# Stick-breaking attention inside a two-layer encoder: from one head at a time to pairs of heads

## The chip, the cores and the metric

One core of a Trainium2 chip runs the whole kernel. The metric is the device time of one execution in microseconds (us); the figure compared is the median of several executions. TensorE is called PE in the profile (PEld is its weight loads), VectorE is DVE, ScalarE is ACT, GpSimd is POOL.

## What is computed

An encoder trunk of two layers over 272 tokens (16 learned ones and 256 frames), 1024 channels, batch 1, all in float32. Each layer is SwiGLU feed-forward, a token mixer, SwiGLU feed-forward, each with an RMSNorm before and after. The mixer of the first layer is stick-breaking attention, the mixer of the second is sliding-window attention. Only the first is touched by the change:

```python
z = einsum('bqhd,bkhd->bhqk', q, k) * HEAD_DIM ** -0.5          # 16 heads of 64 channels
visible = k_pos[None, :] < q_pos[:, None]
log_stay = where(visible, log_sigmoid(-z), 0.0)
log_pass = cumsum(log_stay, axis=3, reverse=True) - log_stay
w = where(visible, exp(log_sigmoid(z) + log_pass), 0.0)
o = einsum('bhqk,bkhd->bqhd', w, v)
```

Before it stands a projection of the 1024 channels to queries, keys and values, behind it an output projection.

## The kernel before, in words

The five engines have one program each; they meet at semaphores. Channels lie on the 128 partitions and tokens along the free axis. The large projections (`in_panel`, `out_panel`) multiply weights that are split into a high and a low part, three matmuls for each block of 128 by 128 (`three`, L887 to L889). All matmuls of the attention itself are plain float32, and each of these calls appears in the profile as two weight loads and two matmuls.

The stick-breaking stage lies between `in_panel` and `out_panel` of the second sub-layer. Its score matrix is kept with keys on the partitions: three blocks of keys (`SB_KEY`), each with the queries that can see them, 272, 144 and 128 columns of which 432 (`SB_W`) are used. For one head:

- TensorE `scores(h)` (L1003 to L1014): three matmuls over the 64 channels of the head, that is, over half of the partitions (`r`, the upper or the lower half by the parity of the head). They write PSUM bank `h % 2` and signal `z_done`. Two calls in flight: it waits until VectorE has read head h-2 (`z_ready`).
- VectorE: `z = SCALE * scores + mask` (L702), then `e = min(-z, z) = -|z|` (L709).
- ScalarE: `e = exp(e)` (L483), `e = ln(1 + e)` (L490).
- VectorE: `sp = max(z, 0) + e` (L718), the softplus of z.
- TensorE `running_sums(h)` (L1016 to L1034): six matmuls of `sp` with a triangle of ones or with ones, over all 128 partitions, into bank `2 + h % 2`; signals `c_done`.
- VectorE: `w = z - sums` (L732); ScalarE: `w = exp(w)` (L487).
- TensorE `values(h)` (L1036 to L1052): three matmuls of `w` with the head's 64 value columns, which fill the upper or lower half of the output partitions of bank `4 + h // 2 % 2`; signals `o_done`.
- For each two heads, ScalarE copies the output to `y_hi` (L494) and VectorE takes the rest `y_lo` (L737), for the output projection.

The order is written out by hand as steps. In step `st` TensorE does `scores(st)`, `running_sums(st - 2)`, `values(st - 4)` (L1066 to L1072). VectorE does `z(st)`, `e(st)`, `sp(st - 1)`, `w(st - 3)`, and in every second step a `y_lo`. ScalarE does `exp(e, st)`, `exp(w, st - 3)`, `ln(st)`, and in every second step a `y_hi`. So the `sp` that `running_sums` of a step reads was made in the step before. Ahead of the steps, TensorE does `scores(0)`, `scores(1)` and 24 transposes of the values (L1062), which ScalarE (L478) and VectorE (L725) copy to `v_tok`.

GpSimd clears the padding columns of `sp` and `w` (L374, L375).

Of the kernel before, what the change touches and what calls it, by code (L numbers as in the profile page):

```python
# [25 lines left out]
P = 128  # L26
# [31 lines left out]
SB_PAD = P - 16  # L58

# [64 lines left out]
def build(nc, x_in, meta_in, norm_g, w_gate, w_up, w_down, sb_w_in, sb_w_out,  # L124
          swa_w_in, swa_sinks, swa_w_out, const_in, out):
    ctx = ExitStack()
    with ctx:
# [36 lines left out]
        with ExitStack() as over:  # L164
            def mix_sb(name, shape, dt=F32):
                return over.enter_context(nc.sbuf_tensor(name, shape, dt))
            qkv = mix_sb("qkv", [P, 3 * KT, L])
            v_tok = mix_sb("v_tok", [P, 3, D])
            z = mix_sb("z", [P, 4, SB_W])
            e = mix_sb("e", [P, 2, SB_W])  # L170
            sp = mix_sb("sp", [P, 2, SB_PAD + SB_W])
            w = mix_sb("w", [P, 3, SB_PAD + SB_W])
        with ExitStack() as over:
# [15 lines left out]
            inv = swa_sb("inv", [P, 2, 2, GROUP])  # L189

# [180 lines left out]
        def _(pool):  # L371

            pool.wait_ge(proj_drained, 1)
            nc.gpsimd.memset(sp[:, :, 0:SB_PAD], 0.0).then_inc(pad_zero, 1)  # L374
            nc.gpsimd.memset(w[:, :, 0:SB_PAD], 0.0).then_inc(pad_zero, 1)  # L375
# [26 lines left out]
        def _(a):  # L402
# [51 lines left out]
            for t in SUBS:  # L454
# [16 lines left out]
                elif t.kind == "sb":  # L471
# [7 lines left out]
                    for st in range(NH + 5):  # L479
                        if st < NH:  # L480

                            a.wait_ge(e_abs, st + 1)
                            nc.scalar.activation(e[:, st % 2], e[:, st % 2], ACT.Exp).then_inc(e_exp, 1)  # L483
                        if 3 <= st < NH + 3:
                            h = st - 3
                            a.wait_ge(d_ready, h + 1)
                            nc.scalar.activation(w[:, h % 3, SB_PAD:], w[:, h % 3, SB_PAD:], ACT.Exp).then_inc(w_ready, 1)  # L487
                        if st < NH:
                            a.wait_ge(e_exp, st + 1)
                            nc.scalar.activation(e[:, st % 2], e[:, st % 2], ACT.Ln, bias=1.0).then_inc(e_ln, 1)  # L490
                        if st >= 5 and (st - 5) % 2 == 1:
                            q = (st - 5) // 2
                            a.wait_ge(o_done, 2 * q + 2)
                            nc.scalar.copy(y_hi[:, q, :], ps[:, 4 + q % 2, 0:L]).then_inc(oh_ready, 1)  # L494
# [87 lines left out]
        def _(v):  # L582
# [52 lines left out]
            for t in SUBS:  # L635
# [58 lines left out]
                if t.kind == "sb":  # L694
                    v.wait_ge(const_in_sem, 16)
                    for st in range(NH + 6):
                        if st < NH:

                            v.wait_ge(z_done, st + 1)
                            if st >= 4:  # L700
                                v.wait_ge(d_ready, st - 3)
                            nc.vector.scalar_tensor_tensor(out=z[:, st % 4], in0=ps[:, st % 2, 0:SB_W],  # L702
                                                           scalar=SCALE, in1=cst("mask_sb"), op0=ALU.mult,
                                                           op1=ALU.add).then_inc(z_ready, 1)
                            v.wait_ge(z_ready, st + 1)
                            if st >= 2:
                                v.wait_ge(sp_ready, st - 1)

                            nc.vector.scalar_tensor_tensor(out=e[:, st % 2], in0=z[:, st % 4], scalar=-1.0,  # L709
                                                           in1=z[:, st % 4], op0=ALU.mult,  # L710
                                                           op1=ALU.min).then_inc(e_abs, 1)
                        if 1 <= st < NH + 1:

                            h = st - 1
                            v.wait_ge(e_ln, h + 1)
                            if h >= 2:
                                v.wait_ge(c_done, h - 1)
                            nc.vector.scalar_tensor_tensor(out=sp[:, h % 2, SB_PAD:], in0=z[:, h % 4], scalar=0.0,  # L718
                                                           in1=e[:, h % 2], op0=ALU.max,
                                                           op1=ALU.add).then_inc(sp_ready, 1)  # L720
                        if 1 <= st < 4:

                            n = 2 * st - 1
                            v.wait_ge(v_turned, n + 1)
                            nc.vector.tensor_copy(v_tok[:, n // 2, 512:1024], ps[:, 2 + n, :]).then_inc(v_saved_d, 1)  # L725
                        if 3 <= st < NH + 3:

                            h = st - 3
                            v.wait_ge(c_done, h + 1)
                            if h >= 3:  # L730
                                v.wait_ge(o_done, h - 2)
                            nc.vector.tensor_tensor(w[:, h % 3, SB_PAD:], z[:, h % 4], ps[:, 2 + h % 2, 0:SB_W],  # L732
                                                    ALU.subtract).then_inc(d_ready, 1)
                        if st >= 6 and (st - 6) % 2 == 0 and (st - 6) // 2 < 8:
                            q = (st - 6) // 2
                            v.wait_ge(oh_ready, q + 1)
                            nc.vector.tensor_tensor(y_lo[:, q, :], ps[:, 4 + q % 2, 0:L],  # L737
                                                    y_hi[:, q, :].bitcast(F32), ALU.subtract).then_inc(ol_ready, 1)
# [144 lines left out]
        def _(pe):  # L883
# [24 lines left out]
            for t in SUBS:  # L908
# [91 lines left out]
                if t.kind == "sb":  # L1000
                    qd = drained_before[t.u]

                    def scores(h):  # L1003
                        r = slice(HD * (h % 2), HD * (h % 2) + HD)
                        if h >= 2:
                            pe.wait_ge(z_ready, h - 1)
                        for n in (2, 0, 1):
                            k0, width = SB_KEY[n], max(L - SB_Q0[n], P)

                            queries = qkv[r, h // 2:h // 2 + 2, :].rearrange("p a t -> p (a t)")  # L1010
                            mm = nc.tensor.matmul(ps[:, h % 2, SB_COL[n]:SB_COL[n] + width],  # L1011
                                                  qkv[r, KT + h // 2, k0:k0 + P],
                                                  queries[:, SB_Q0[n]:SB_Q0[n] + width], start=True, stop=True)
                        mm.then_inc(z_done, 1)  # L1014

                    def running_sums(h):  # L1016

                        pe.wait_ge(sp_ready, h + 1)
                        if h >= 2:
                            pe.wait_ge(d_ready, h - 1)  # L1020
                        else:

                            pe.wait_ge(v_saved_a, 1)
                            pe.wait_ge(v_saved_d, 1)
                        for n, m in ((2, 2), (0, 0), (0, 1), (0, 2), (1, 1), (1, 2)):

                            at, src = SB_COL[n] + SB_Q0[m] - SB_Q0[n], SB_PAD + SB_COL[m]
                            back = SB_PAD if m == 2 and n < 2 else 0
                            width = max(L - SB_Q0[m], P) - back
                            mm = nc.tensor.matmul(ps[:, 2 + h % 2, at - back:at + width],  # L1030
                                                  cst("tri" if m == n else "ones"),
                                                  sp[:, h % 2, src - back:src + width],
# [225 lines left out]
```

## Time and profile before

| what | us |
|---|---|
| median of three executions | 1123.28 |
| lowest and highest of them | 1122.22, 1127.62 |
| span of the profiled execution (first to last instruction) | 1119.9 |
| TensorE busy in that span | 1080.2 |
| stick-breaking stage, from its first matmul to the first of the output projection | 295.85 to 363.87 |

The page gives no time of the profiled execution beside its span; the median of the executions is 3.4 us above that span. Times in the rows are microseconds from the first instruction of the profiled execution.

### The profile page before, as it was taken

What the parts mean: (1) busy time and instruction counts of PE and PEld (TensorE: products, weight loads), DVE (VectorE), ACT (ScalarE), POOL (GpSimd) and SP (SyncE); (2) the same over time, 40 slices, a digit from 0 to 9 for tenths busy, and PEclk for the clock granted to TensorE, in tenths of its full rate; (3) what the DMA queues carried; (4) which work ended last, traced back from release to release, by engine and by line L of the source; (5) the groups of instructions that cost most, each with busy time, mean ns of one, the idle gap of its engine ahead of it and who ended that gap; (6) DMA issues with size and microseconds to landing.
All of it is one profiled execution on the core that took longest, in us unless ns stands there. A gap on an engine that the chain in (4) does not pass through costs nothing.

```text
span 1119.9 us, 20564 instructions
## 1 busy us (share of the span) xinstructions
PE 1080.2 (96%) x8367; PEld 1045.7 (93%) x8367; DVE 653.1 (58%) x875; ACT 503.3 (45%) x710; POOL 10.9 (1%) x17
## 2 busy tenths in 40 slices
PE   7999999999999999999999999999997999999997
PEld 6999999899877899999998999999896789999996
DVE  5575553576565477555437765544687667755433
ACT  4554343444344455444334544433553746544422
POOL 0000000000000000000000000000011000000000
PEclk9999999999999999999999999999998999999998
DMA  7576555436300427654452665545340054765531
GB/s 232 177 229 188 166 173 188 150 114 225 113 1 1 151 77 225 186 187 156 183 186 78 189 211 165 186 169 170 113 152 37 4 186 125 236 202 187 188 113 38
DMA packets 125720, 169.62 MB, mean 151 GB/s; under 512 B 2674, under 2 KB 111442, under 8 KB 125666
## 3 DMA queue, kind: packets, MB, share of 16 engines
q1 hardware_dynamic: 125232, 167.78, 46.1%
q10 hardware_dynamic: 434, 1.06, 0.3%
q8 instruction: 41, 0.67, 0.3%
q14 instruction: 13, 0.11, 0.0%
HBM read 167.78 MB, written 1.05 MB: 151 GB/s over the span
## 4 chain that ended last, share of the span: by engine, by line
PE 93%; DVE 4%; ACT 1%; DMA 1%; issue 0%; SPq 0%; DVEq 0%; ACTq 0%
PE ps L887 25%; PE ps L889 25%; PE ps L888 25%; PE ps L1030 3%; PE ps L931 3%; PE ps L933 2%; PE ps L940 2%; PE ps L1048 1%; PE ps L1011 1%; PE ps L1113 1%; DVE w_lo L591 1%; PE ps L1182 1%; PE ps L1099 1%; DMA raw<-in_ffn_w_gate_dram 1%; PE ps L1084 1%; DVE scaled L851 0%
## 5 line engine op out<-in xcount | busy, mean ns | idle before, releaser
L414 ACT CAST w_hi<-raw 128x1024 fp32r<-128x1024 f32 x316 | 315.6, 1047 | 443.7 <-PE ps L889 337.6
L591 DVE TENSOR_TENSOR w_lo<-raw,w_hi 128x1024 fp32r<-128x1024 f32 x316 | 375.1, 1229 | 236.2 <-ACT w_hi L414 235.6
L887 PE MATMUL ps<-y_hi,w_lo 128*128 128x272 f32 (+1 forms) x1600 | 461.4, 288 | 2.9 <-DVE y_lo L737 1.0
L889 PE MATMUL ps<-y_lo,w_hi 128*128 128x272 f32 (+1 forms) x1600 | 459.8, 287 | 0.0
L888 PE MATMUL ps<-y_hi,w_hi 128*128 128x272 f32 (+1 forms) x1600 | 458.1, 286 | 0.0
L887 PEld LDWEIGHTS ps<-y_hi,w_lo 128*128 128x128 f32 x1600 | 301.3, 188 | 4.2 <-issue 3.5
L888 PEld LDWEIGHTS ps<-y_hi,w_hi 128*128 128x128 f32 x1600 | 301.4, 188 | 0.3
L889 PEld LDWEIGHTS ps<-y_lo,w_hi 128*128 128x128 f32 x1600 | 301.4, 188 | 0.0
L888 PE MATMUL ps<-h_hi,w_hi 128*128 (+2 forms) x704 | 201.6, 286 | 0.0
L887 PE MATMUL ps<-h_hi,w_lo 128*128 (+2 forms) x704 | 201.6, 286 | 0.0
L889 PE MATMUL ps<-h_lo,w_hi 128*128 (+2 forms) x704 | 200.9, 285 | 0.0
L887 PEld LDWEIGHTS ps<-h_hi,w_lo 128*128 128x128 f32 x704 | 132.7, 188 | 0.0
L889 PEld LDWEIGHTS ps<-h_lo,w_hi 128*128 128x128 f32 x704 | 132.5, 188 | 0.0
L888 PEld LDWEIGHTS ps<-h_hi,w_hi 128*128 128x128 f32 x704 | 132.4, 188 | 0.0
L931 PE MATMUL ps<-y_hi,w_lo 128*128 128x272 f32 (+1 forms) x224 | 60.2, 298 | 11.7 <-DVE y_hi L867 11.7
L650 DVE TENSOR_TENSOR hid<-act,ps 128x544 f32<-128x544 f32 (+1 forms) x44 | 31.2, 710 | 66.1 <-PE ps L889 66.1
L645 DVE TENSOR_TENSOR act<-ps,rms_inv 128x544 f32<-128x544 f32 (+1 forms) x44 | 31.5, 716 | 53.3 <-PE ps L889 49.1
L933 PE MATMUL ps<-y_hi,w_hi 128*128 128x272 f32 (+1 forms) x224 | 59.3, 294 | 0.0
L931 PEld LDWEIGHTS ps<-y_hi,w_lo 128*128 128x128 f32 x224 | 44.0, 196 | 14.0 <-DVE y_hi L867 13.8
L933 PEld LDWEIGHTS ps<-y_hi,w_hi 128*128 128x128 f32 x224 | 44.0, 196 | 0.0
L422 ACT ACTIVATE y_hi<-xT,gains 128x272 fp32r<-128x272 f32 (+1 forms) x43 | 22.3, 521 | 33.7 <-DVE xT L859 30.3
L940 PE MATMUL ps<-y_lo,w_hi 128*128 128x272 f32 (+1 forms) x224 | 35.6, 292 | 0.0
(106 smaller groups left out, 712.9 us busy)
## 6 DMA issues: line engine op xcount, KB each, us to landing
raw<-in_ffn_w_gate_dram SPq DMA_DIRECT2D x44, 1024.0 KB, 5.4
raw<-in_ffn_w_up_dram SPq DMA_DIRECT2D x44, 1024.0 KB, 5.4
raw<-in_ffn_w_down_dram SPq DMA_DIRECT2D x44, 1024.0 KB, 4.9
raw<-in_sb_w_in_dram SPq DMA_DIRECT2D x12, 1024.0 KB, 5.2
raw<-in_swa_w_in_dram SPq DMA_DIRECT2D x6, 1024.0 KB, 5.1
raw<-in_sb_w_out_dram SPq DMA_DIRECT2D x4, 1024.0 KB, 4.9
raw<-in_swa_w_out_dram SPq DMA_DIRECT2D x4, 1024.0 KB, 5.0
sq<-in_x_dram SPq DMA_DIRECT2D x1, 1024.0 KB, 5.8
```

The lines of the kernel that those rows point to most:

```text
L414: nc.scalar.copy(w_hi[:, g % SLOTS, part], raw[:, g % RAW_SLOTS, part]).then_inc(hi_ready, 1)
L422: nc.scalar.activation(y_hi[:, d, t0:L], xT[:, d, t0:L], ACT.Copy, scale=gains[:, SUBS[b].pre + d:SUBS[b].pre + d + 1]).then_inc(yh_ready, 1)
L591: nc.vector.tensor_tensor(w_lo[:, g % SLOTS, part], raw[:, g % RAW_SLOTS, part], w_hi[:, g % SLOTS, part].bitcast(F32), ALU.subtract).then ...
L645: nc.vector.tensor_tensor(act[:, j % 2, :, t0:L], ps[:, b0:b0 + 2, t0:L], spread(rms_inv, 2, t0), ALU.mult).then_inc(gate_ready, 1)
L650: nc.vector.tensor_tensor(hid[:, j % 2, :, t0:L], act[:, j % 2, :, t0:L], ps[:, b0:b0 + 2, t0:L], ALU.mult).then_inc(h_ready, 1)
L887: nc.tensor.matmul(dst, w_lo[:, slot, pc], yh, start=first, stop=False)
L888: nc.tensor.matmul(dst, w_hi[:, slot, pc], yh, start=False, stop=False)
L889: return nc.tensor.matmul(dst, w_hi[:, slot, pc], yl, start=False, stop=last)
L931: nc.tensor.matmul(dst, w_lo[:, g % SLOTS, pc], y_hi[:, k, t0:L], start=(k == 0), stop=False)
L933: nc.tensor.matmul(dst, w_hi[:, g % SLOTS, pc], y_hi[:, k, t0:L], start=False, stop=False)
L940: nc.tensor.matmul(ps[:, BANK_IN[i][c], t0:L], w_hi[:, g % SLOTS, pc], y_lo[:, k, t0:L], start=False, stop=False)
L1030: mm = nc.tensor.matmul(ps[:, 2 + h % 2, at - back:at + width], cst("tri" if m == n else "ones"), sp[:, h % 2, src - back:src + width], st ...
```

## The change

The stage works on pairs of heads (`PAIRS` is 8). `scores(p)` issues the three score matmuls of both heads in turn, one in the upper and one in the lower half of the input partitions, into banks 0 and 1; there is one such pair of banks. `running_sums(p)` does the six matmuls of one head and then the six of the other, into banks 2 and 3 or 6 and 7 in turn. `values(p)` alternates between the two halves of the output partitions. Each elementwise instruction takes both heads, 864 columns. `-|z|` on VectorE is replaced by `Abs` on ScalarE, and the exponential takes its sign through `scale=-1.0`. `e` now lies over `sq`, and `w` over `fT`, which are free in this stage; `z` has three places, `sp` and `w` two. The three VectorE copies of the values stand in step 0.

The orders of one step become: TensorE `scores(st)`, `running_sums(st - 1)`, `values(st - 2)`; VectorE `z(st)`, `sp(st - 1)`, `w(st - 2)`, `o_low(st - 3)` (that is `y_lo`); ScalarE `abs(st)`, `exp(st)`, `ln(st)`, `exp(w, st - 2)`, `y_hi(st - 3)`.

```diff
-            z = mix_sb("z", [P, 4, SB_W])
-            e = mix_sb("e", [P, 2, SB_W])
-            sp = mix_sb("sp", [P, 2, SB_PAD + SB_W])
-            w = mix_sb("w", [P, 3, SB_PAD + SB_W])
+            z = mix_sb("z", [P, 3, 2, SB_W])
+            sp = mix_sb("sp", [P, 2, 2, SB_PAD + SB_W])
...
+        e = sq[:].rearrange("p a b -> p (a b)")[:, 0:4 * SB_W].rearrange("p (r a n) -> p r a n", r=2, a=2)
+        w = fT[:].rearrange("p a b -> p (a b)").rearrange("p (r a n) -> p r a n", r=2, a=2)
...
@@ ScalarE
-                    for st in range(NH + 5):
+                    for st in range(PAIRS + 4):
+                        if st < PAIRS:
+                            a.wait_ge(z_ready, st + 1)
+                            if st >= 2:
+                                a.wait_ge(sp_ready, st - 1)
+                            nc.scalar.activation(e[:, st % 2], z[:, st % 3], ACT.Abs).then_inc(e_abs, 1)
                             a.wait_ge(e_abs, st + 1)
-                            nc.scalar.activation(e[:, st % 2], e[:, st % 2], ACT.Exp).then_inc(e_exp, 1)
+                            nc.scalar.activation(e[:, st % 2], e[:, st % 2], ACT.Exp, scale=-1.0).then_inc(e_exp, 1)
                             a.wait_ge(e_exp, st + 1)
                             nc.scalar.activation(e[:, st % 2], e[:, st % 2], ACT.Ln, bias=1.0).then_inc(e_ln, 1)
+                        if 2 <= st < PAIRS + 2:
+                            p = st - 2
+                            a.wait_ge(d_ready, p + 1)
+                            nc.scalar.activation(w[:, p % 2, :, SB_PAD:], w[:, p % 2, :, SB_PAD:], ACT.Exp)\
+                                .then_inc(w_ready, 1)
...
@@ VectorE
-                    for st in range(NH + 6):
+                    for st in range(PAIRS + 4):
+                        if st < PAIRS:
                             v.wait_ge(z_done, st + 1)
...
+                            nc.vector.scalar_tensor_tensor(out=z[:, st % 3], in0=ps[:, 0:2, 0:SB_W],
+                                                           scalar=SCALE, in1=mask, op0=ALU.mult,
                                                            op1=ALU.add).then_inc(z_ready, 1)
...
+                        if 1 <= st < PAIRS + 1:
+                            p = st - 1
+                            v.wait_ge(e_ln, p + 1)
+                            if p >= 2:
+                                v.wait_ge(c_done, p - 1)
+                            nc.vector.scalar_tensor_tensor(out=sp[:, p % 2, :, SB_PAD:], in0=z[:, p % 3], scalar=0.0,
+                                                           in1=e[:, p % 2], op0=ALU.max,
                                                            op1=ALU.add).then_inc(sp_ready, 1)
+                        if 2 <= st < PAIRS + 2:
+                            p = st - 2
+                            v.wait_ge(c_done, p + 1)
...
+                            nc.vector.tensor_tensor(w[:, p % 2, :, SB_PAD:], z[:, p % 3], ps[:, b0:b0 + 2, 0:SB_W],
                                                     ALU.subtract).then_inc(d_ready, 1)
+                        if 3 <= st < PAIRS + 3:
+                            o_low(st - 3)
...
@@ TensorE
-                    def scores(h):
-                        r = slice(HD * (h % 2), HD * (h % 2) + HD)
-                        if h >= 2:
-                            pe.wait_ge(z_ready, h - 1)
+                    def scores(p):
+                        if p >= 1:
+                            pe.wait_ge(z_ready, p)
                         for n in (2, 0, 1):
                             k0, width = SB_KEY[n], max(L - SB_Q0[n], P)
+                            for half in range(2):
+                                r = slice(HD * half, HD * half + HD)
+                                queries = qkv[r, p:p + 2, :].rearrange("p a t -> p (a t)")
+                                mm = nc.tensor.matmul(ps[:, half, SB_COL[n]:SB_COL[n] + width],
+                                                      qkv[r, KT + p, k0:k0 + P],
+                                                      queries[:, SB_Q0[n]:SB_Q0[n] + width], start=True, stop=True)
                         mm.then_inc(z_done, 1)
...
+                    def running_sums(p):
+                        pe.wait_ge(sp_ready, p + 1)
...
+                        for half in range(2):
+                            for n, m in ((2, 2), (0, 0), (0, 1), (0, 2), (1, 1), (1, 2)):
...
+                    def values(p):
+                        pe.wait_ge(w_ready, p + 1)
...
                         for n in range(3):
...
+                            for half in range(2):
+                                r, h = slice(HD * half, HD * half + HD), 2 * p + half
+                                mm = nc.tensor.matmul(ps[r, 4 + p % 2, SB_Q0[n] - back:L],
+                                                      v_tok[:, n, HD * h:HD * h + HD],
+                                                      w[:, p % 2, half, src - back:src + L - SB_Q0[n]],
+                                                      start=(n == 0), stop=(n == 2), skip_group_check=True)
...
-                    for st in range(2, NH + 4):
-                        if st < NH:
+                    for st in range(1, PAIRS + 2):
+                        if st < PAIRS:
                             scores(st)
-                        if 2 <= st < NH + 2:
-                            running_sums(st - 2)
-                        if 4 <= st:
-                            values(st - 4)
+                        if 1 <= st < PAIRS + 1:
+                            running_sums(st - 1)
+                        if 2 <= st:
+                            values(st - 2)
```

## Rows read from the trace of the kernel before

Instructions whose operand columns show `128x432` work on 432 columns of one head. A window's busy time is followed by the number of instructions that overlap it.

**Rows 1.** The page: busy time of each engine; the chain that ended last.
```profile
PE 1080.2 (96%) x8367; PEld 1045.7 (93%) x8367; DVE 653.1 (58%) x875; ACT 503.3 (45%) x710; POOL 10.9 (1%) x17
...
PE 93%; DVE 4%; ACT 1%; DMA 1%; issue 0%; SPq 0%; DVEq 0%; ACTq 0%
```

**Rows 2.** Steady stage: us; busy us of PE, PEld, DVE, ACT, POOL; clock; DMA, GB/s.
```profile
307.50:347.70 40.20, 40.07 (x242) 32.18 (x241) 25.07 (x47) 17.51 (x37) 0.00 (x0) 1.00 0.00 1
```

**Rows 3.** The chain of waits through the stage: start us, us, what.
```profile
295.85 1.49 PE ps L1011 x10
...
302.75 1.85 PE ps L1030 x12
...
331.70 1.12 PE ps L1011 x6
332.83 1.81 PE ps L1030 x12
334.64 1.06 PE ps L1048 x6
```

**Rows 4.** Timeline of one steady head, all engines.
```profile
331.63 1.19 PE L1011 MATMUL ps<-qkv 64*128 64x128 f32 x6
...
332.86 0.61 DVE L702 SCALAR_TENSOR_TENSOR z<-ps,const 128x432 f32<-128x432 f32 x1 [1.72 <-PE ps L1011]
...
334.03 0.60 DVE L718 SCALAR_TENSOR_TENSOR sp<-z,e 128x432 f32<-128x432 f32 x1
...
334.55 0.60 DVE L732 TENSOR_TENSOR w<-z,ps 128x432 f32<-128x432 f32 x1
```

**Rows 5.** Score matmuls (L1011): one head alone, then the two first heads.
```profile
331.62:332.76 1.14, 1.12 (x6) 0.89 (x6) 1.00 0.06 14
295.84:297.27 1.43, 1.42 (x12) 1.24 (x12) 1.00 0.98 340
```

**Rows 6.** The other layer's score matmuls (L1084) of its two first heads.
```profile
844.29:844.85 0.56, 0.55 (x8) 0.55 (x9) 1.00 0.00 0
```

**Rows 7.** Value matmuls (L1048) of heads 13 and 14, one behind the other.
```profile
360.32:361.68 1.36, 1.35 (x11) 1.08 (x12) 1.00 0.00 0
```

**Rows 8.** Groups by shape: elementwise instructions of 432 and 1088 columns.
```profile
L702 DVE SCALAR_TENSOR_TENSOR z<-ps,const 128x432 f32<-128x432 f32 x16 | 9.7, 605 | 12.8 <-PE ps L1011 12.7
...
L608 DVE TENSOR_TENSOR fT<-fT 128x1088 f32<-128x1088 f32 x5 | 6.5, 1292 | 6.2 <-ACT fT L429 6.2
...
L429 ACT ACTIVATE fT<-xT 128x1088 f32<-128x1088 f32 x10 | 10.5, 1098 | 0.0
L487 ACT ACTIVATE w<-w 128x432 f32<-128x432 f32 x16 | 9.0, 562 | 10.2 <-DVE w L732 10.2
```

**Rows 9.** Timeline of the stage's first and last microseconds.
```profile
297.27 2.84 PE L1062 MATMUL ps<-const,qkv 128*128 128x128 f32 x24
...
299.71 0.58 ACT L478 COPY v_tok<-ps 128x512 f32<-128x512 f32 x1 [0.29 <-PE ps L1062]
300.05 1.19 PE L1011 MATMUL ps<-qkv 64*128 64x128 f32 x6
...
362.86 0.39 ACT L494 CAST y_hi<-ps 128x272 fp32r<-128x272 f32 x1 [0.95 <-PE ps L1048]
...
363.28 0.44 DVE L737 TENSOR_TENSOR y_lo<-ps,y_hi 128x272 fp32r<-128x272 f32 x1 [0.90 <-ACT y_hi L494]
...
363.87 0.36 PE L887 MATMUL ps<-y_hi,w_lo 128*128 128x272 f32 x1 [1.04 <-DVE y_lo L737]
```

**Rows 10.** TensorE after two of four equal pauses (the others: 221.64, 801.28).
```profile
392.31 0.40 PE L931 MATMUL ps<-y_hi,w_lo 128*128 128x272 f32 x1 [2.36 <-DVE y_hi L867]
...
596.10 0.59 PE L931 MATMUL ps<-y_hi,w_lo 128*128 128x272 f32 x1 [2.36 <-DVE y_hi L867]
```

**Rows 11.** Granted clock (the column PEclk) after those two pauses.
```profile
392.00:396.00 4.00, 3.69 (x29) 1.00 0.00 0
597.00:598.00 1.00, 1.00 (x6) 0.50 0.00 0
```

More of the change, by code:

```diff
@@ L58 @@
 SB_PAD = P - 16
+PAIRS = NH // 2
+C_BANK = [2, 6]
 SW_TOKENS = [list(range(144)), list(range(META)) + list(range(80, L))]
@@ L373, in _ @@
             pool.wait_ge(proj_drained, 1)
-            nc.gpsimd.memset(sp[:, :, 0:SB_PAD], 0.0).then_inc(pad_zero, 1)
-            nc.gpsimd.memset(w[:, :, 0:SB_PAD], 0.0).then_inc(pad_zero, 1)
+            for r in range(2):
+                nc.gpsimd.memset(sp[:, r, :, 0:SB_PAD], 0.0).then_inc(pad_zero, 1)
+                nc.gpsimd.memset(w[:, r, :, 0:SB_PAD], 0.0).then_inc(pad_zero, 1)
             pool.wait_ge(const_in_sem, 16)
@@ L695, in _, with o_low @@
                     v.wait_ge(const_in_sem, 16)
-                    for st in range(NH + 6):
-                        if st < NH:
+                    v.wait_ge(pad_zero, 4)
+                    def o_low(q):
+                        v.wait_ge(oh_ready, q + 1)
+                        nc.vector.tensor_tensor(y_lo[:, q, :], ps[:, 4 + q % 2, 0:L],
+                                                y_hi[:, q, :].bitcast(F32), ALU.subtract).then_inc(ol_ready, 1)
+                    mask = cst("mask_sb").unsqueeze(1).broadcast_to([P, 2, SB_W])
@@ L721, in _ @@
[L721 to L732, printed above, removed]
-                                                    ALU.subtract).then_inc(d_ready, 1)
@@ L734, in _ @@
[L734 to L738, printed above, removed]
+                        if st == 0:
+                            for n in (1, 3, 5):
+                                v.wait_ge(v_turned, n + 1)
+                                nc.vector.tensor_copy(v_tok[:, n // 2, 512:1024], ps[:, 2 + n, :]).then_inc(v_saved_d, 1)
@@ L1014, in scores @@
                         mm.then_inc(z_done, 1)
[L1016 to L1020, printed above, removed]
-                        else:
[L1023 to L1032, printed above, removed]
-                                                  start=(m == n), stop=(m == 2), skip_group_check=True)
+                    def running_sums(p):
+                        pe.wait_ge(sp_ready, p + 1)
+                        if p >= 2:
+                            pe.wait_ge(d_ready, p - 1)
+                        else:
+                            pe.wait_ge(v_saved_a, 1 + 2 * p)
+                            pe.wait_ge(v_saved_d, 1 + 2 * p)
+                        for half in range(2):
+                            for n, m in ((2, 2), (0, 0), (0, 1), (0, 2), (1, 1), (1, 2)):
+                                at, src = SB_COL[n] + SB_Q0[m] - SB_Q0[n], SB_PAD + SB_COL[m]
+                                back = SB_PAD if m == 2 and n < 2 else 0
+                                width = max(L - SB_Q0[m], P) - back
+                                mm = nc.tensor.matmul(ps[:, C_BANK[p % 2] + half, at - back:at + width],
+                                                      cst("tri" if m == n else "ones"),
+                                                      sp[:, p % 2, half, src - back:src + width],
+                                                      start=(m == n), stop=(m == 2), skip_group_check=True)
```

57 lines of the change are left out of this document (14 added, 43 removed).

## The prediction

> **What bounds the kernel now.** I read the page first: TensorE is busy for 1080.2 of 1119.9 us and makes up 93% of the chain that ended last [rows 1]. Inside the stage that the change touches, the windows say the same: in the 40.20 us from 307.50, TensorE is busy 40.07, VectorE 25.07 and ScalarE 17.51 [rows 2]. The chain of waits there is nothing but three TensorE blocks in turn, scores 1.12 us, running sums 1.81, values 1.06, so 3.99 us a head and 7.98 for two [rows 3]. No engine keeps it waiting. So removing TensorE work from this stage pays, as long as TensorE stays the bound. That is the question here.
>
> **What a block costs.** A float32 call is two matmuls. Scores stream 2 x (128 + 272 + 144) = 1088 columns, sums 2 x (128 + 272 + 144 + 128 + 144 + 128) = 1888. Both use 128 weight columns, so 1.81 - 1.12 = 0.69 us for 800 columns gives 0.86 ns a column, and 0.18 us of each block (1.12 - 0.94) is the fixed price of entering it: the first weights and the change of array shape [rows 3].
>
> **Part 1: do the two halves run together?** The old kernel already shows it wherever two heads of different halves stand side by side. The first two heads' scores, 12 matmuls, take 1.43 us where one head takes 1.14, though they aren't even alternated [rows 5]. In the other layer, 8 matmuls of two heads (1408 columns, 1.21 us one after the other) fit in 0.56 [rows 6]. Column halves do the same: 11 of the 12 value matmuls of heads 13 and 14 have begun within 1.36 us, where one head takes 1.06 [rows 3, 7], the second beginning only when the first was half through. Alternated, I take a pair as one head plus 0.02 us: scores 1.14, values 1.08. The bounds are 0.00 and, if alternation undoes it, 0.94 more each. The sums use the whole array, so a pair is 0.18 + 2 x 1.63 = 3.44. TensorE's own work for a pair falls from 7.98 to 5.66 us.
>
> The Trainium skill, "TensorEngine Tiling (Array Packing)", section Theoretical Speedup, promises up to twice the rate for dimensions of 64 or less; the rows above agree for short stretches. Its section on the PSUM bottleneck warns that the evacuation of PSUM isn't sped up with it; by the first rule alone the stage would lose 2.3 us a pair, by the second nothing need be gained, and what follows decides from rows.
>
> **Part 2: the elementwise instructions.** From 432 to 1088 columns a VectorE instruction goes from 605 to 1292 ns, 1.05 ns a column; ScalarE from 562 to 1098, 0.82 a column [rows 8]. At 864 columns that makes 1.06 and 0.92 us. The upper bound is twice the price at 432, 1.21 and 1.12. The trace has no Abs; I take it at the price of the exponential, 0.92, the nearest row; below it can't be under its columns alone, 864 x 0.82 ns = 0.71, above I let it be twice as dear, 1.84 (the cover named below hides 0.8 of that). VectorE then does three of 1.06 and a `y_lo` of 0.44 for a pair, 3.6 us; ScalarE four of 0.92 and a copy of about 0.4, 4.1. Neither is near 7.98 by sum.
>
> **Part 3: the order, which moves a wait onto the path.** Before, `running_sums(st - 2)` read an `sp` of the previous step. Now TensorE's step is `scores(st)`, `running_sums(st - 1)`, and VectorE makes `sp(st - 1)` in the same step, behind `z(st)`, which needs `scores(st)`. With one pair of score banks nothing can be issued ahead. So each step has a serial path through VectorE while TensorE, with `values(st - 2)` and the next scores queued behind, stands still:
> - scores begin to `z` begins: 1.23 us for one head (331.63 to 332.86) [rows 4], 1.25 for a pair;
> - `z`: 1.06 less the 0.08 by which VectorE starts an instruction that doesn't need the last result before that one ends (0.52 between starts of 0.60 us instructions) [rows 4]: 0.98;
> - `sp`: 1.06, and 0.15 until TensorE starts (363.28 + 0.44 to 363.87) [rows 9];
> - sums 3.44, values 1.08.
>
> Together 7.96 us for a pair, against 7.98 before. The 2.3 us that the array saves is what it now waits.
>
> Is anything else later? ScalarE gets `z` at 1.25 + 1.06 = 2.31 us of the step, does abs, exp, ln by 5.1 and the exp of `w(st - 2)` by 6.1 (its input is ready at 4.3). TensorE reaches the values at 6.9. Cover of 0.8 us: it hides Abs, and the upper bound of four ScalarE instructions, 4 x 0.2, just uses it up. The two pad clearings on GpSimd become four, long before the stage; the output copies, `y_lo` (done by 6.9) and the buffer waits all refer to earlier steps. DMA and the weight conversions don't change. All cost nothing.
>
> **The ends of the stage.** Scores of one pair instead of two heads one behind the other: 1.14 for 1.42 (295.85 to 297.27), so the transposes and ScalarE's value copies come 0.28 earlier, the third ends at 300.01 [rows 3, 9]. Abs, exp, ln of the wide pair take 3 x 0.94 to 302.83, `sp(0)` to 303.90, the first sums start at 304.05 (before: 302.75 [rows 3]) and end at 307.49. Six full steps of 7.96: 355.25. The last `sp` stands behind ScalarE's and VectorE's work of that step and lets the sums begin at 355.4; they end at 358.9. Then `w` is written by 360.1, its exponential ends at 361.0, values 1.08 + 0.11 of drain end at 362.3, and the output halves take the old 1.01 (362.86 to 363.87 [rows 9]): 363.3 against 363.87.
>
> **The sum:** -0.6 us on the span of 1119.9. The median of the runs, 1123.28, is 3.4 above that span; kept so, I get 1122.7. In this kernel about 0.5%, 5.6 us, can be told from no change.
>
> **Bounds.** Wide instructions at the upper price add 0.3 a step, 2.1 in all; a second head that lags by 0.1 in each block adds 1.6; exact concurrency saves 0.3. So the forecast's own range is 1119 to 1127.
>
> **The rivals.**
> - *TensorE stays the bound, the full gain.* This needs `sp(st - 1)` ready when `scores(st)` ends. Against it is VectorE's written order. Even then ScalarE's 6.1 us (above) plus values 1.08 would set a step of 7.2, 0.8 less than before: seven times makes 5.3, with the 0.6 of the ends about 1117; were that cover absent too, 2.3 x 7 less 1.3 of the later start is 15, about 1108. Chance 0.06.
> - *The clock, slower.* TensorE now stands about 2.2 us in each of seven steps. After pauses of 2.36 us the old trace shows both outcomes: at 392.31 the granted clock stayed 1.00 (2.4 GHz), after 596.10 it was 0.50 (1.2 GHz) [rows 10, 11]. For it: a similar pause seven times. Against: those pauses come after and before thin work, these between 5.6 us of dense work. At half clock a step's columns (0.94 + 3.26 + 0.94) cost 5.1 us more; with a third of each step at 0.50, 1.7 x 7 = 12 us, 1134.7. It decides from four such stretches on; one or two stay within "no change" (1124 to 1126). Chance 0.08.
> - *Alternation doesn't overlap.* If weights of one half held up matmuls of the other, or two halves writing one PSUM bank (values) took turns, both blocks double: 1.9 x 8 = 15 us, 1138. One of the two alone gives 1130. Rows 5 to 7 speak against it. Chance 0.06.
> - *Abs is dear* (it changes function tables, or is slower than exp by over 0.8 us): all above that lands on the path, 1 us more makes 8, about 1131. The Trainium skill, "ScalarE: Activation LUTs", in its part on table sets, says abs is in every set; no row here shows it. Chance 0.03.
>
> **How the numbers follow.** The forecast has 0.77: faster 0.06 (first rival), slower 0.08 + 0.06 + 0.03 = 0.17, no change the forecast's own 0.77. The range goes from 1118.5, just outside the forecast's lower bound, to 1130, which takes in a few slow stretches and half of the third rival.
>
> **What would show it.** If right: a step of 8.0 us; 12 score matmuls of a pair in 1.1 to 1.2 us and 12 value matmuls in about 1.1; TensorE idle for about 2.2 us before each first sum, released by VectorE's `sp`; TensorE's busy share in the steady part falling from 99.7% to about 73%; `z` and `sp` at about 1.06 us; first sums near 304.0. Wrong if the pause is absent, if value matmuls wait for ScalarE's `w`, if PEclk is under 1.00 in the stage, or if a pair's scores take over 1.5 us.

## The result and the profile after

The changed kernel takes 1130.48 us in the median of eleven executions (1128.67 to 1133.97), the kernel before 1123.28 beside it: a ratio of 1.0057, 95% interval 1.0039 to 1.0075. It is slower, by 0.6%, where I had forecast no change (1122.7, range up to 1130.0). A second comparison gave 1.0068 (1.0042 to 1.0093). Executions of the kernel before lie in two groups, near 1122 and near 1128 us, and the profiled one, whose span is 1119.9 where 1119.8 belongs to 1121.59 us in its second profile, is of the lower.

The page of the changed kernel: busy time, the granted clock in 40 slices, and the chain by engine.

```profile
PE 1073.6 (95%) x8367; PEld 1043.5 (92%) x8367; DVE 641.6 (57%) x835; ACT 506.4 (45%) x694; POOL 11.2 (1%) x19
...
PEclk9999999999998999999999999999998999999998
...
PE 92%; DVE 5%; ACT 1%; issue 1%; DMA 1%; SPq 0%; DVEq 0%; ACTq 0%
```

TensorE is busy 6.6 us less than before [rows 1] and still the span grew from 1119.9 to 1128.7 us. Windows over the stage (us, then busy us and count of PE, PEld, DVE, ACT, POOL, then granted clock, DMA share, GB/s):

```profile
307.00:351.40 44.40, 33.78 (x256) 28.78 (x255) 16.70 (x19) 19.15 (x25) 0.00 (x0) 0.92 0.00 1
...
322.00:324.00 2.00, 2.00 (x9) 1.77 (x8) 0.44 (x1) 1.08 (x2) 0.00 (x0) 0.50 0.00 0
```

Where TensorE was busy all the time before [rows 2], it is now busy 76% of it. And the clock column is no longer 1.00 throughout. The pause stands in brackets in the timeline of TensorE, 2.12 us in six steps; ahead of the first sums it is 2.94:

```profile
320.14 5.16 PE L1039 MATMUL ps<-sp,const 128*128 128x128 f32 x24 [2.12 <-DVE sp L732]
```

The chain of waits shows both, here for a step in which the clock fell and the next, in which it did not (start us, us, what; the operand names `fT` and `sq` in these views are `w` and `e`, which lie over them):

```profile
316.89 1.15 PE ps L1019 x12
...
318.10 0.94 issue
319.04 1.06 DVE sp L732
...
320.14 5.16 PE ps L1039 x24
...
326.38 1.15 PE ps L1019 x12
...
327.69 0.83 issue
328.52 1.06 DVE sp L732
...
329.63 3.50 PE ps L1039 x24
```

After the scores (1.15 us) TensorE stands until VectorE has made `z` (the piece called "issue" lies inside it) and `sp` (1.06). Then come 24 matmuls of the sums, 3.50 us at full clock, 5.16 us where the clock fell, and the values, 1.07. From one block of sums to the next it is 9.49 us with a fall (320.14 to 329.63) and 7.82 without (329.63 to 337.45, the next such piece). The wide instructions, in the groups by shape, VectorE first (line engine op, operands, count, busy us, mean ns, idle before):

```profile
L719 DVE SCALAR_TENSOR_TENSOR z<-ps,const 128x864 f32<-128x864 f32 x8 | 8.5, 1057 | 24.2 <-PE ps L1019 24.2
L732 DVE SCALAR_TENSOR_TENSOR sp<-z,sq 128x864 f32<-128x864 f32 x8 | 8.4, 1049 | 0.7 <-ACT sq L494 0.7
```

```profile
L490 ACT ACTIVATE sq<-z 128x864 f32<-128x864 f32 x8 | 7.4, 922 | 27.3 <-DVE z L719 27.3
```

And the 12 score matmuls and 12 value matmuls of one pair, in windows that hold just them:

```profile
334.12:335.28 1.16, 1.15 (x12) 0.91 (x12) 1.00 0.05 14
```

```profile
333.05:334.13 1.08, 1.07 (x12) 0.73 (x12) 1.00 0.00 0
```

Each has a fellow in the rows of before: 1.14 us for the six scores of one head [rows 5] and 1.06 for its values [rows 3].

**Where 8.8 us of span went.** The stage begins 1.68 us later (297.53 for 295.85), is 3.2 longer (297.53 to 368.74, 71.2, for 68.0), and what follows takes 3.9 more (759.9 for 756.0). In the stage three of the seven sums blocks behind a pause took 5.16 instead of 3.50, 5.0 us together; without them it would have been 66.2, that is 1.8 shorter than before. Outside it the code is the same and the clock differs: there are four more stretches at half clock, of 1.4 to 1.7 us each. One stands at the start of the output projection, three behind pauses of 2.36 us like those of [rows 10]: of these four pauses one was followed by half clock before, and all four are now. Two of them, of the changed kernel and then of the kernel before, whose code runs 8 us earlier by the second (us, PE busy, PEclk, DMA share, GB/s):

```profile
222.00:226.00 4.00, 4.00 (x21) 0.57 0.00 0
...
810.00:813.00 3.00, 3.00 (x15) 0.51 0.00 0
```

```profile
222.00:226.00 4.00, 4.00 (x34) 1.00 0.00 0
...
801.00:805.00 4.00, 3.72 (x29) 1.00 0.00 0
```

### The profile page after: what moved, and what is told of

It reads as the page before. It is cut to its first block, busy times and chain, and to the rows that moved or that the text cites. A ratio compares the mean times of both kernels' runs of the same rounds, so it can differ in the third digit from the quotient of the medians.

```text
span 1128.7 us, 20467 instructions
## 1 busy us (share of the span) xinstructions
PE 1073.6 (95%) x8367; PEld 1043.5 (92%) x8367; DVE 641.6 (57%) x835; ACT 506.4 (45%) x694; POOL 11.2 (1%) x19
## 3 DMA queue, kind: packets, MB, share of 16 engines
q10 hardware_dynamic: 434, 1.06, 0.3%
HBM read 167.78 MB, written 1.05 MB: 150 GB/s over the span
## 4 chain that ended last, share of the span: by engine, by line
PE 92%; DVE 5%; ACT 1%; issue 1%; DMA 1%; SPq 0%; DVEq 0%; ACTq 0%
PE ps L894 25%; PE ps L895 25%; PE ps L896 25%; PE ps L1039 3%; PE ps L938 3%; PE ps L947 3%; PE ps L940 2%; PE ps L1122 1%; DVE w_lo L600 1%; PE ps L1191 1%; PE ps L1108 1%; DMA raw<-in_ffn_w_gate_dram 1%; PE ps L1019 1%; PE ps L1057 1%; DVE sp L732 1%
## 5 line engine op out<-in xcount | busy, mean ns | idle before, releaser
L896 PE MATMUL ps<-y_lo,w_hi 128*128 128x272 f32 (+1 forms) x1600 | 460.4, 288 | 0.0
L1039 PE MATMUL ps<-sp,const 128*128 128x144 f32 (+1 forms) x192 | 33.0, 338 | 15.7 <-DVE sp L732 15.7
L1039 PEld LDWEIGHTS ps<-sp,const 128*128 128x128 f32 x192 | 29.7, 220 | 19.1 <-DVE sp L732 17.2
```

Source lines behind the costliest of these rows:

```text
L896: return nc.tensor.matmul(dst, w_hi[:, slot, pc], yl, start=False, stop=last)
L1039: mm = nc.tensor.matmul(ps[:, C_BANK[p % 2] + half, at - back:at + width], cst("tri" if m == n else "ones"), sp[:, p % 2, half, src - back ...
```

## The experiments

Theories: (1) VectorE's `z` and `sp`, put in one step with the sums that read `sp`, hold TensorE in each step and eat what the halves save; (2) the pauses this makes let the clock fall, and that alone turns "no change" into "slower". Rivals: the wide instructions or the alternation don't perform; the clock differs by chance. In each edit below the lines belong to the changed kernel unless it is said otherwise. Each comparison has its own executions of the kernel before; medians of these were 1127.57 us beside the runs with eight matmuls, with `sp` first, and with both orders changed (with and without alternation), 1123.36 beside those with four matmuls and with the values later, 1123.28 beside the last. The highest of them comes from more executions near 1128, so times of different groups can be compared to about 4 us only, and the ratios of the first group flatter by up to 0.4%.

### Eight matmuls in the pause

```diff
                     def running_sums(p):
-                        pe.wait_ge(sp_ready, p + 1)
...
+                        if p < PAIRS - 1:
+                            for _ in range(8):
+                                nc.tensor.matmul(ps[:, C_BANK[p % 2], 0:P], cst("ident"), cst("ident"),
+                                                 start=True, stop=True, skip_group_check=True)
+                        pe.wait_ge(sp_ready, p + 1)
```

> The changed kernel, with eight extra float32 matmuls of 128 by 128 columns (of a constant, into the bank that the next running sums overwrite) put between the scores and the running sums of each of the first seven pairs, in the 2.12 us in which TensorE waits for sp. They take 8 x 0.22 + 0.18 = 1.9 us, so they fit in the pause. Theory 1 (the loss is the clock: three of the seven sums blocks ran at 0.50 and took 5.16 us instead of 3.50): with the pause filled no stretch of the stage is at 0.50, all sums blocks take 3.3 to 3.5, the stage shrinks from 71.2 us to about 66, and the kernel is some 5 us faster than the changed one, 1125 to 1126, that is within 0.3% of the kernel before. Theory 2 (the order is the loss, the clock only happens to differ between two executions): the stage stays near 71 or grows, the kernel stays at 1130 or above.

Measured: 1122.6 us, 0.9970 (0.9951 to 0.9989) of the kernel before. The stage of the filled kernel as one window, with PEclk 1.00, and a step of its chain of waits:

```profile
297.40:363.70 66.30, 62.36 (x521) 54.14 (x521) 29.60 (x35) 33.37 (x44) 0.00 (x0) 1.00 0.03 9
```

```profile
320.05 3.50 PE ps L1043 x24
...
327.87 3.50 PE ps L1043 x24
```

More work made the kernel 7.9 us faster than the changed one by the medians (by the ratios, 1.0057 and 0.9970, some 0.9%). All sums blocks take 3.50 or less, the step is still 7.82 (320.05 to 327.87), the stage 66.3. So theory 2 holds inside the stage: its 5.0 us are the clock. Another 3 us, more than expected, came outside: 1.4 in the output projection, whose first microseconds ran at half clock in the changed kernel and not here, and about 1 in the attention of the second layer, where half clock lasted 10.2 us there and 6.8 here. That those also follow from the pauses in the stage is not shown. For the pauses of 2.36 us between the sub-layers the filled kernel speaks against it. Windows behind three of them, the first, the third and the fourth:

```profile
222.00:225.00 3.00, 3.00 (x14) 0.50 0.00 0
...
597.50:600.50 3.00, 3.00 (x14) 0.50 0.00 0
803.00:805.00 2.00, 2.00 (x11) 0.50 0.00 0
```

All four are followed by half clock, as in the changed kernel, though the pauses of the stage's steps are filled.

### Four matmuls

> The changed kernel with four instead of eight extra matmuls in each of the seven pauses: 1.05 us of each pause of 2.12 filled, 1.07 left. Theory 1 (the clock falls after pauses of some 2 us and not after those of 1 us; the run with VectorE's sp first had pauses of 1.41 us and no fall inside the stage): no stretch at 0.50 in the stage, the stage takes 66 us, the time is that of the run with eight, 1121 to 1124. Theory 2 (each pause must be filled almost wholly): one or more sums blocks of 5.2 us, 1124 to 1130.

Measured: 1122.5 us, 0.9990 (0.9975 to 1.0006). The first block of sums and the second, in the chain of waits:

```profile
305.62 5.16 PE ps L1043 x24
...
314.04 3.50 PE ps L1043 x24
```

The six pauses of 1.04 us were followed by no fall. The first pause, 1.85 us because it is longer to start with, was followed by one, and its block took 5.16. The time agrees with theory 1 of the expectation, its "no stretch in the stage" doesn't: one is there.

### VectorE's `sp` first

In VectorE's step the block `sp(st - 1)` is moved ahead of the block `z(st)`.

> The changed kernel with one move on VectorE: sp(st-1) ahead of z(st) in each step; d and o_low behind, ScalarE's order as it is. Theory (the serial path scores, z, sp holds TensorE): the 2.12 us pause ahead of the running sums goes. Behind it ScalarE is late: z ends at 2.3 us of the step, abs, exp, ln at 5.1, exp of w at 6.0, so the values wait about 1.5 us and a step takes 7.2 instead of 7.83 us; the stage is about 66 to 67 us where the clock holds. Rival (TensorE was held by something else than VectorE's order): step stays at 7.8.

Measured: 1120.28 us, 0.9948 (0.9927 to 0.9968). One step on the timeline:

```profile
331.65 3.50 PE L1039 MATMUL ps<-sp,const 128*128 128x128 f32 x24
...
334.77 0.92 ACT L494 ACTIVATE sq<-sq 128x864 f32<-128x864 f32 x1
335.60 0.91 ACT L498 ACTIVATE fT<-fT 128x864 f32<-128x864 f32 x1
...
336.55 0.68 PE L1057 MATMUL ps<-fT,v_tok 128*64 128x272 f32 x4 [1.41 <-ACT fT L498]
```

The pause ahead of the sums is gone and one of 1.41 us stands ahead of the values, behind ScalarE's logarithm and the exponential of `w`. Steps take 7.11 us. Theory 1 of the two above holds, and so does the first rival of the prediction as far as it went: with `sp` early, ScalarE sets the step. It was worked out as 7.2. The stage takes 62.7 us (297.63 to 360.31), without a stretch at half clock, and not the 66 to 67 expected, which a step of 7.2 for 7.83 already undercuts.

### Both orders changed

Also `w(st - 2)` ahead of `z(st)` on VectorE, and the exponential of `w` ahead of abs, exp and ln on ScalarE (in words; `d` is the subtraction that writes `w`):

```diff
 VectorE step:  -z(st), sp(st-1), d(st-2), o_low(st-3)   +sp(st-1), d(st-2), z(st), o_low(st-3)
 ScalarE step:  -abs, exp, ln (st), exp w (st-2), y_hi   +exp w (st-2), abs, exp, ln (st), y_hi
```

> The changed kernel with VectorE's step in the order sp(st-1), d(st-2), z(st), o_low(st-3) and ScalarE's exp of w(st-2) ahead of abs, exp, ln of the step. Theory (the array halves do save 2.3 us a pair, and only the orders of the two elementwise engines hid it): TensorE runs its three blocks back to back, 1.15 + 3.42 + 1.07 = 5.65 us a step, no stretch at 0.50, the stage takes about 54 us, and the kernel 1108 to 1111, 1.1 to 1.3% faster than the kernel before. Rival (ScalarE or VectorE becomes the bound): a step of 6.5 to 7.2 us, 1115 to 1118.

Measured: 1116.96 us, 0.9919 (0.9893 to 0.9946). The rival was right, with a step of 6.51 us. The chain of waits through the steady steps has no TensorE in it:

```profile
321.56 1.05 DVE sp L720
322.61 0.96 DVE fT L730
323.57 0.98 DVE z L737
324.57 0.93 ACT sq L495
325.53 0.93 ACT sq L497
326.48 0.92 ACT sq L499
327.41 0.28 ACT y_hi L503
...
328.07 1.05 DVE sp L720
```

It is a loop: `sp`, `w` and `z` on VectorE, three functions on ScalarE, then `y_hi` and `y_lo`, and only then the next `sp`. I had summed each engine but not followed that loop round.

### The same without alternation

```diff
-                        for n in (2, 0, 1):
-                            for half in range(2):
+                        for half in range(2):
+                            for n in (2, 0, 1):
```

(likewise in the values)

> The run before it (orders changed), but with the scores and values of the two heads of a pair one head behind the other instead of alternating. Theory (a second head is admitted once the first is half through, as in the old trace: 1.43 us for two heads' scores, about 1.6 for two heads' values): scores and values cost 0.3 and 0.5 more a pair, a step takes 6.4 us, the kernel about 6 us more than with alternation. Rival (alternation brings nothing beyond what the engine's own reordering gives): no difference over 1 us. Rival 2 (halves only run together when alternated): 0.9 more each, 15 us more.

Measured: 1117.67 us, 0.9921 (0.9890 to 0.9953), no difference to the run before where 6 us were expected. This told nothing about alternation: with it TensorE had about 0.9 us a step to spare behind the loop (6.51 less 5.6), and without it TensorE needs 6.46 a step, just what the loop takes. So it was tried again where TensorE is the bound.

### The values one step later

```diff
-                    for st in range(1, PAIRS + 2):
+                    for st in range(1, PAIRS + 3):
...
-                        if 2 <= st:
-                            values(st - 2)
+                        if 3 <= st:
+                            values(st - 3)
 VectorE step:  +sp(st-1), o_low(st-4), z(st), d(st-2)
 ScalarE step:  +y_hi(st-4), abs, exp, ln (st), exp w (st-2)
```

> The changed kernel with TensorE's values one step later (values(st-3)), so that exp of w is off every path; VectorE in the order sp(st-1), o_low(st-4), z(st), d(st-2), ScalarE in the order y_hi(st-4), abs, exp, ln(st), exp of w(st-2). Theory (the halves save 2.3 us a pair; the run with orders changed was held at 6.51 us a step by a loop sp, d, z, abs, exp, ln, y_hi, y_lo): the loop is now sp, z, abs, exp, ln, about 4.9 us, TensorE is the bound again with 1.15 + 3.42 + 1.07 = 5.65 us a step and no pauses, the stage takes 52 to 54 us, the kernel about 1110 us. Rival (another wait shows up in its place): a step over 6.2 us, 1114 or more.

Measured: 1115.03 us, 0.9920 (0.9891 to 0.9950). The steady step in the chain of waits:

```profile
322.69 3.43 PE ps L1039 x24
326.12 1.07 PE ps L1057 x12
327.20 1.13 PE ps L1019 x12
328.32 3.43 PE ps L1039 x24
```

TensorE is the bound again, in blocks of 3.43, 1.07 and 1.13, a step of 5.63 us (322.69 to 328.32): the 2.3 us a pair that the array halves save, now on the path. The total is 5 us above what I expected and in the range of the rival, though not for its reason, a step over 6.2. The stage took 56.9 and not 52 to 54: the first and the last full step are still serial (6.2 us of scores, `z`, three functions and `sp` before their sums), and the first sums, behind a pause of 2.94, took 5.16 at half clock. The output projection began at half clock too, after pauses of 1.98 and 1.08 on either side of the last values.

### The same without alternation

> The run before it with scores and values of a pair not alternated but one head behind the other. Now TensorE is the bound, so what alternation gives shows in full: scores 1.45 and values 1.58 as measured in the earlier run without alternation, a step of 6.46 us, the stage about 6 us longer and the kernel 1116. If alternation were worth nothing: the same time as with it. If TensorE weren't the bound: a difference under 2 us.

Measured: 1117.97 us, 0.9941 (0.9920 to 0.9962). A steady step in the chain of waits:

```profile
321.19 1.45 PE ps L1019 x10
322.64 3.43 PE ps L1039 x24
326.07 1.58 PE ps L1057 x10
327.65 1.45 PE ps L1019 x10
```

Scores 1.45 for 1.13 and values 1.58 for 1.07, a step of 6.46: 0.83 us a step is what alternation brings. Without it the second head's first matmul begins 0.33 us after the first head's in the scores and 0.52 in the values; with it, 0.01. The stage of this profile takes 61.7 us (296.06 to 357.79) for 56.9, with one stretched block in both. Of these 4.9 us only 2.9 show between the medians, where I expected 6; the profile with alternation had two stretches of half clock outside the stage that this one had not.

### The first pair's functions ahead of the copies

```diff
-                    for n in range(0, 6, 2):
-                        a.wait_ge(v_turned, n + 1)
-                        nc.scalar.copy(v_tok[:, n // 2, 0:512], ps[:, 2 + n, :]).then_inc(v_saved_a, 1)
+                    save_v(0)
...
+                            if st == 0:
+                                save_v(2)
+                                save_v(4)
```

> The run with values one step later, and in step 0 ScalarE copies only the first of its three value blocks ahead of abs, exp and ln of the first pair, the two others behind. Theory: the first sums begin 1.7 us earlier (the pause ahead of them shrinks from 2.94 to about 1.3 us), and the kernel is 1.7 us faster, about 1108.5, 1.3 to 1.7% faster than the kernel before. Rival (the copies then hold up pair 1 or the first values): less than 1 us.

Measured: 1111.16 us, 0.9889 (0.9868 to 0.9910), the fastest of all, 1.1% below the kernel before. TensorE's timeline where the first sums begin, with the pause before them in brackets:

```profile
302.56 0.72 PE L1044 MATMUL ps<-sp,const 128*128 128x128 f32 x3 [1.38 <-DVE sp L725]
```

The pause ahead of them is 1.38 instead of 2.94 us, and this block ran at full clock. The stage takes 53.7 us (296.09 to 349.83), 3.1 less than in the profile without this edit: 1.5 by the pause and 1.7 by the clock. The medians differ by 3.9, more than the 1.7 expected; besides the stretch in the stage the profile without this edit had one at 221.55 us that this one had not. With the run before it above its expectation, the 1108.5 expected here was missed all the same.

### The order alone, on the kernel before

The kernel before, head by head:

```diff
-                        if 2 <= st < NH + 2:
-                            running_sums(st - 2)
+                        if st == 2:
+                            running_sums(0)
+                        if 2 <= st < NH + 1:
+                            running_sums(st - 1)
...
-                        if 3 <= st < NH + 3:
-                            h = st - 3
+                        if 2 <= st < NH + 2:
+                            h = st - 2
```

> The kernel before, one head at a time, with only the distance between engines changed as in the changed kernel: TensorE does running_sums(st-1) instead of (st-2), so it reads an sp that VectorE makes in the same step behind z and e; w is made one step earlier too. Theory (the shorter distance alone puts a serial VectorE path on every step): scores to z 1.23, z 0.63, e 0.52, sp 0.60, 0.15 to TensorE, sums 1.81, values 1.06, so 6.0 us a head against 4.0, TensorE pausing about 1.9 us in each of 15 heads; 28 to 30 us more, 1151, and above that whatever the clock adds. Rival (the distance is harmless, the wide elementwise instructions make the wait): no change, 1123.

Measured: 1163.1 us, 1.0330 (1.0288 to 1.0371). One head in which the clock held (366.89 to 372.83, the next such piece, 5.94 us), in the chain of waits:

```profile
366.89 1.88 PE ps L1030 x12
368.78 1.07 PE ps L1048 x6
369.85 1.14 PE ps L1011 x6
```

The pause is 1.86 us (1.9 expected), with instructions of the old width. So the distance in steps makes the wait, where VectorE makes `sp` behind `z`, and not the wide instructions; with `sp` first, as shown above, the same distance holds nothing up. The stage takes 107.1 us (297.56 to 404.66) for 68.0. Of these 39 us, 13 pauses make steps 1.95 longer each, 25 in all, and nine stretches of half clock inside the stage account for most of the rest.

### The changed kernel without alternation

> The changed kernel with scores and values of a pair one head behind the other instead of alternating. In the order of the changed kernel both blocks lie on the serial path of a step, so it costs what it cost where TensorE was the bound: 0.3 in the scores, 0.5 in the values, a step of 8.65 us where the clock holds and 6 us more in all, 1134 to 1138. If the pause absorbed it: the same time as the changed kernel.

Measured: 1136.82 us, 1.0099 (1.0063 to 1.0135): 6.3 above the changed kernel's first median and 2.9 above its second, which was taken beside it, so that by the intervals the two can't be told apart. A step in the chain of waits:

```profile
346.29 5.07 PE ps L1039 x24
351.36 1.58 PE ps L1057 x10
352.94 1.47 PE ps L1019 x10
```

Scores are 1.47 and values 1.58, so the steps are longer by 0.83. All seven sums blocks behind a pause ran in part at half clock, so the expected step of 8.65 us was never seen.

### Both kernels once more

> The changed kernel once more, with a second profile. The clock theory says that steps without a fall are the same to 0.02 us (7.83) and that the stretches at 0.50 lie elsewhere or differ in number: two to seven of the sums blocks at 5.2 us, stage 69 to 78 us, time 1128 to 1135. Rival (the same three blocks every time): identical.

Measured: 1133.96 us (1128.77 to 1136.76), span 1135.0. Two sums blocks of this profile's chain of waits, 19 and 38 us behind the first:

```profile
324.50 5.16 PE ps L1039 x24
...
343.47 3.50 PE ps L1039 x24
```

Five of the seven blocks behind a pause were stretched, four to 5.1 or 5.2 and the first to 6.49, against three before; steps without a fall are again 7.83. The stage took 75.8 us, 4.6 more than in the first profile, and 9.5 us of it lie in stretched blocks, so 66.3 without.

> The kernel before once more, for a second profile: its executions fall in two groups, near 1122 and near 1128. If the clock makes them, the stage has no stretch at 0.50 in either, and the number of pauses between the sub-layers (four of 2.36 us) that are followed by 0.50 differs with the time, each costing 1.5 to 1.7 us.

Measured: 1121.59 us, and a profile like the first: no half clock in the stage, one of the four pauses between sub-layers followed by it, at the same place (596 us). It is from the lower group, like the first, so what the upper one is made of was not seen.

## Why the prediction was wrong

**The blocks and halves: right.** Scores of a pair 1.15 (forecast 1.14), values 1.07 (1.08), sums 3.50 and, without a pause in front, 3.43 (3.44). TensorE's own work for a pair did fall from 7.98 to 5.63, as the steady step of the later version shows.

**The elementwise instructions: right.** 1.06 and 1.05 for a forecast of 1.06, 0.92 for 0.92, Abs like the others at 922 ns. The Trainium skill, "ScalarE: Activation LUTs", in its part on table sets, says that abs is in every table set; this case's traces agree, with nine table loads in either kernel and none of them in the stage.

**The order: right.** The pause is 2.12 us (2.2 forecast) and the step 7.82 (7.96), the first sums began 8.04 us after the first scores (8.2). Had the clock held, the stage would have been 66.2 us and not the 67.4 I worked out, 1.8 shorter than before; the 66.3 of the filled kernel bears that out. The array's gain went into waiting for VectorE, as said. The Trainium skill warns in "TensorEngine Tiling (Array Packing)", in its section on the PSUM bottleneck, that tiling doesn't speed up the evacuation of PSUM. What held TensorE here was indeed behind VectorE's reading of the scores, but it was no bottleneck of evacuation: with other orders and the same instructions the step fell to 5.63 us.

**The clock: the step that failed.** The sum had no term for the clock. I gave "a similar pause seven times" a chance of 0.08, because the earlier pauses stood between thin work and these between dense, and nothing on record bore that reason out. Measured: three of seven such pauses were followed by half clock in one execution, five of seven in the other, and the experiment that changed nothing but to fill them took all of it out of the stage. The term missing from the sum measured 5.0 to 9.5 us in the stage, and in the first of the two executions about 1.4 more in the output projection behind it. The mechanism was a rival; its price for each stretch, 1.7 us, was measured as 1.66. The record I had, one fall in four pauses of 2.36 us [rows 10, 11], was no reason for rareness: one in four, times seven at 1.7, would have put 3 us into the sum, 1125.7, and the upper end of the range with it above what was measured. The bound "it decides from four stretches on" counted only those inside the stage.

**The base outside the stage.** I also kept everything outside the stage as it was in the one profile before. There one of the four pauses of 2.36 us was followed by half clock, and in the changed kernel all four, 1.5 to 1.7 us more for each of three. This part is not explained by the change: all four were followed by half clock in the filled kernel too, with `sp` first, with both orders changed and with the values one step later; three of them in the two without alternation that follow these and in the last and fastest; two with four matmuls.

**What stays open.** Why these stretches outside the stage, one of them 75 us ahead of it in code that is the same, were there in nearly all other kernels and not in the two profiles of the kernel before, both of its lower group. With the output projection, and 0.6 us won back in the second layer's attention, they make up 5.6 of the 8.8 us of span. The executions of the kernel before spread from 1121.5 to 1129.6, so part of it may be which execution was profiled: the medians are 7.2 us apart, the two spans 8.8.

The version that beats both is the last in the row of orders: 1111.16 us.

## What to carry to other kernels

When engines hand work to each other in steps, count in how many steps a result must be ready, and at which place of its producer's step it is made, before counting how much faster its consumer gets: a distance of one step instead of two, with the result made behind another one of the same step, put the producer on the path and ate nearly all 2.3 us a pair here. Follow each loop through the engines round once, with its own sum, beside the sum for each engine. And a pause of TensorE costs more than its length where pauses like it were followed by half clock even once: put the expected number of stretches into the sum; filling them with matmuls that nobody reads is a cheap test.

## What I had not expected

- Two heads in different halves of the array overlap in part without any alternation in the program: the scores of two take 1.45 us where one head takes 1.14, the values 1.58 where one takes 1.06.
- Inside the stage TensorE kept full clock behind pauses of 1.04 us (six of six) and of 1.41 (five of five). Behind pauses of 1.86 us it fell in 8 of 13 cases, behind those of 2.12 in 3 and 4 of 6 in the two profiles of the changed kernel and in 6 of 6 without alternation. Behind the first pause, 2.94 us in five profiles, it fell in two. A limit in length doesn't follow from these: the output projection began at half clock in the changed kernel behind pauses of 1.03 and 1.08.
- Fifty-six matmul calls whose result nobody reads took 7.9 us off the changed kernel, by the medians of two comparisons.
